# Sparse attention taken by pairs of heads, its last 16 queries gathered over heads, and the top-k rounds spread over query, key and value slots

## The chip, the cores and the metric

The kernel runs on one core of a Trainium2 chip. The metric is the device time of one execution in microseconds (us). The engines that matter here are TensorE (PE in the rows; PEld are its weight loads), VectorE (DVE), ScalarE (ACT), GpSimdE (POOL) and the queue of SyncE (SP) that fetches weights. ScalarE also issues DMAs from its own queue (ACTq).

## The reference

A network of three parts: a hybrid layer, a differential attention with a feed-forward network, and a sparse attention (DSA) with a feed-forward network. Width 1024, 512 tokens, and 16 "meta" tokens put ahead of them from the second part on, so 528 tokens. The change touches only the sparse attention:

```python
q, k, v, qi, ki, wi = jnp.split(h @ w_in, DSA_SPLITS, axis=-1)
q = apply_rope(q.reshape(B, T, 16, 64), cos, sin) * (64 ** -0.5)
k = apply_rope(k.reshape(B, T, 16, 64), cos, sin)
...
raw = jnp.einsum('bqhd,bkd->bqhk', qib, ki).astype(f32) * (64 ** -0.5)
score = jnp.einsum('bqhk,bqh->bqk', jax.nn.relu(raw), wb)
score = jnp.where(causal & (k_pos < 16)[None, :], BIG_SCORE, score)
score = jnp.where(causal, score, -jnp.inf)
top_val, top_idx = lax.top_k(score, 128)       # n_keys // 4
...                                            # keys and values at top_idx
s = jnp.where(valid[:, None], s, -jnp.inf)
p = jax.nn.softmax(s, axis=-1)
o = jnp.einsum('bhqj,bqjhd->bqhd', p, vs)
```

An indexer scores all keys for each query, the 128 best keys are taken, and 16 heads of 64 channels attend to them. Then comes the output projection, and later the second feed-forward network.

## The kernel before

**Weights in slots.** Each projection is a stream of slots: 128 output channels by 1024 inputs, 512 KB. SyncE fetches a slot into `raw`; ScalarE rounds it to `w_hi` (line 895); the rest, `w_lo`, is the difference, made by VectorE (line 1131) or, for the slots S_DSA + 7 to the first of the output projection, by GpSimdE (line 867). TensorE takes three products for each half of the tokens and each of eight input tiles (lines 551 to 553), 48 matmuls for a slot. Two slots of `w_hi` and `w_lo` exist, so ScalarE waits for the slot two back before it writes the next one (`ahead`). Three pairs of PSUM banks take the results.

**The stage ahead of the attention.** Slots S_DSA + 0 to 6 are the indexer's query, key and weights; then the indexer's scores are accumulated in `sel`, one tile of 128 queries at a time. After that TensorE runs slots 7 to 30: 8 slots of queries, 8 of keys, 8 of values. Queries and keys are made in pairs of slots: `rope` (lines 1180 to 1188) reads both from PSUM on VectorE, and `scatter` (line 939) moves the result by eight DMAs of ScalarE's queue to where its heads belong. A slot can start only when the `rope` that reads the same pair of banks three slots back is done (`dsa_free`). Value slots are scaled by VectorE (`vch`, line 1199), transposed by TensorE (line 584), and copied to `vtok` by VectorE (lines 1194, 1195).

**The top-k.** Queries stand in `TILES`: four tiles of 128 and a last one of 16, so tile n has keys(n) = 256, 384, 512, 528 keys for n = 1 to 4 (n = 0 selects nothing). One round, `take_eight(r)`, finds the eight largest of each row (MAX8, line 1476) and replaces them by a mark (line 1477); 16 rounds take 128 keys, and a final instruction (line 1480) turns the marks into a bias of 0 or -1e30. The four tiles make 64 rounds, all on VectorE, eight after each of the eight `rope`s, tile by tile in the order 1, 2, 3, 4. The value slots come when all are done.

**The attention** goes through 80 units, `HEAD_UNITS`: 16 heads by five tiles. The queries stand in `qz`, padded with zeros to 128 rows so that a head can be taken against the keys of two heads in `kz`; GpSimdE zeroes it (line 877). Of unit u TensorE makes the scores (line 596; the last tile in two halves, lines 598 and 599), VectorE scales them, adds the bias and takes the maximum (line 1309) and its negative (line 1311), ScalarE takes the exponential and its sum (line 1009), VectorE divides (lines 1317, 1319), TensorE transposes the probabilities (line 608), ScalarE copies them out (`copy_pt`, lines 946 to 949), TensorE multiplies by the values (line 618: for both heads of a pair, 128 columns), and ScalarE copies the head's 64 rows to `oT` (line 1015). TensorE computes the scores three units ahead of the transposes, VectorE and ScalarE work two units ahead. After every pair of heads ScalarE rounds `oT` to `o_hi` and GpSimdE makes the rest `o_lo` (line 873), which the output projection needs. A float32 product of TensorE appears as two instructions in the trace, a transpose as one.

The differential attention, earlier in the same kernel, takes its heads by pairs already: its scores (line 644) use 64 rows of the array for each head of a pair; its transposes are line 663 and its values line 672. The first layer has products with 64 columns of weights for each of two heads (line 1688).

## Time and profile before

| | us |
|---|---|
| median of 3 runs | 2063.96 (2061.88 to 2067.09) |
| profiled execution, its own time | 2064.38 |
| its span, first to last instruction | 2062.5 |
| TensorE busy | 1864.3 (90%) |
| VectorE busy | 1244.1 (60%) |
| ScalarE busy | 680.1 (33%) |
| GpSimdE busy | 101.4 (5%) |
| share of TensorE in the chain that ended last | 78% |
| share of VectorE in that chain | 16% |

The span is what the profile sees of the execution; 1.9 us of the execution's own time lie outside it. "Busy" is a union of instructions that overlap. The clock column of a row is the TensorE clock granted in that stretch: 1.00 is 2.4 GHz and 0.50 is 1.2 GHz, its two levels. Two lines of the chain are the rounds of the top-k: line 1477 with 2% of the span and line 1476 with 2%.

### The profile page before, as it was taken

How to read it: one execution, taken by the hardware profiler on the slowest of the kernel's cores; microseconds unless marked ns; L12 is line 12 of the kernel's file. 1: busy time of each engine (PE TensorE's matmuls, PEld its weight loads, DVE VectorE, ACT ScalarE, POOL GpSimd, SP SyncE). 2: the span in 40 equal slices, each digit the busy share in tenths (PEclk: the TensorE clock that was granted, in tenths of full speed). 3: DMA queues.
4: the chain of work that ended last, by engine and by line, in shares of the span. 5: the costliest groups of instructions: out<-in, count | busy, mean ns of one | idle time of the engine just before them, and what ended most of it. 6: DMA issues, size and time to landing. Idle time of an engine off the chain costs nothing.

```text
span 2062.5 us, 34799 instructions
## 1 busy us (share of the span) xinstructions
PE 1864.3 (90%) x14740; PEld 1659.1 (80%) x14740; DVE 1244.1 (60%) x2283; ACT 680.1 (33%) x1273; POOL 101.4 (5%) x53
## 2 busy tenths in 40 slices
PE   7999568979998859999999996987999999999996
PEld 3777458858994439999999995887766899999885
DVE  5256645437546654878773356797466477777534
ACT  3354222332115543222222223211477432222221
POOL 0000002000000000000000020232200000000000
PEclk9999769999997979999999998998999999999998
DMA  8332200022530002323333331342100123333331
GB/s 308 120 92 83 92 1 3 13 82 86 142 93 11 1 0 73 103 92 92 88 89 101 95 100 53 86 112 82 53 1 1 34 91 93 92 93 92 101 103 62
DMA packets 51290, 160.39 MB, mean 78 GB/s; under 512 B 8256, under 2 KB 9280, under 8 KB 51008
## 3 DMA queue, kind: packets, MB, share of 16 engines
q1 hardware_dynamic: 43648, 147.35, 22.9%
q10 hardware_dynamic: 7488, 10.82, 2.1%
q8 instruction: 117, 1.92, 0.4%
q14 instruction: 37, 0.30, 0.0%
HBM read 146.32 MB, written 2.10 MB: 72 GB/s over the span
## 4 chain that ended last, share of the span: by engine, by line
PE 78%; DVE 16%; issue 2%; ACT 1%; DMA 1%; ACTq 1%; SPq 0%; DVEq 0%
PE banks L551 17%; PE banks L552 17%; PE banks L553 16%; PE banks L1779 3%; PE banks L1567 3%; PE banks L1569 3%; PE banks L1568 3%; PE banks L618 3%; DVE arena L1477 2%; DVE top L1476 2%; PE banks L672 2%; PE banks L596 1%; PE banks L608 1%; DMA ring<-in_weights 1%; PE banks L644 1%
## 5 line engine op out<-in xcount | busy, mean ns | idle before, releaser
L551 PE MATMUL banks<-hn_hi,w_hi 128*128 128x264 f32 (+1 forms) x2288 | 658.9, 288 | 31.3 <-DVE hn_lo L1138 14.9
L552 PE MATMUL banks<-hn_lo,w_hi 128*128 128x264 f32 (+1 forms) x2288 | 653.1, 285 | 0.0
L553 PE MATMUL banks<-hn_hi,w_lo 128*128 128x264 f32 (+1 forms) x2288 | 652.3, 285 | 0.0
L895 ACT ACTIVATE w_hi<-raw 128x1024 fp32r<-128x1024 f32 x207 | 219.4, 1061 | 887.8 <-PE banks L553 836.3
L551 PEld LDWEIGHTS banks<-hn_hi,w_hi 128*128 128x128 f32 x2288 | 436.8, 191 | 35.8 <-issue 20.4
L552 PEld LDWEIGHTS banks<-hn_lo,w_hi 128*128 128x128 f32 x2288 | 438.2, 192 | 0.1
L553 PEld LDWEIGHTS banks<-hn_hi,w_lo 128*128 128x128 f32 x2288 | 435.6, 190 | 0.0
L1131 DVE TENSOR_TENSOR w_lo<-raw,w_hi 128x1024 fp32r<-128x1024 f32 x181 | 221.6, 1225 | 197.0 <-ACT w_hi L895 196.9
L551 PE MATMUL banks<-a_hi,w_hi 128*128 128x264 f32 (+1 forms) x528 | 169.1, 320 | 1.6 <-DVE u_in L1361 0.8
L552 PE MATMUL banks<-a_lo,w_hi 128*128 128x264 f32 (+1 forms) x528 | 169.4, 321 | 0.0
L553 PE MATMUL banks<-a_hi,w_lo 128*128 128x264 f32 (+1 forms) x528 | 169.4, 321 | 0.0
L551 PEld LDWEIGHTS banks<-a_hi,w_hi 128*128 128x128 f32 x528 | 99.5, 188 | 9.4 <-DVE u_in L1361 1.0
L553 PEld LDWEIGHTS banks<-a_hi,w_lo 128*128 128x128 f32 x528 | 99.3, 188 | 7.6
L552 PEld LDWEIGHTS banks<-a_lo,w_hi 128*128 128x128 f32 x528 | 99.1, 188 | 7.8
L1120 DVE TENSOR_TENSOR ring_r<-ring,ring_r 128x1024 fp32r<-128x1024 f32 x33 | 40.5, 1226 | 86.7 <-ACT ring_r L890 86.6
L1568 PE MATMUL banks<-h_r,ring_r 128*128 128x512 f32 x200 | 79.2, 396 | 0.0
L551 PE MATMUL banks<-o_hi,w_hi 128*128 128x264 f32 (+1 forms) x256 | 73.2, 286 | 0.0
L552 PE MATMUL banks<-o_lo,w_hi 128*128 128x264 f32 (+1 forms) x256 | 73.1, 285 | 0.0
L553 PE MATMUL banks<-o_hi,w_lo 128*128 128x264 f32 (+1 forms) x256 | 72.8, 284 | 0.0
L867 POOL TENSOR_TENSOR w_lo<-raw,w_hi 128x1024 fp32r<-128x1024 f32 x26 | 62.4, 2400 | 183.8 <-ACT w_hi L895 183.8
L618 PE MATMUL banks<-arena 128*128 128x128 f32 (+2 forms) x480 | 68.4, 272 | 0.5 <-ACT arena L1015 0.5
L1373 DVE SCALAR_TENSOR_TENSOR u_c<-u_in,cols,u_c 128x528 f32<-128x528 f32 (+1 forms) x88 | 67.0, 761 | 3.1
(370 smaller groups left out, 2955.7 us busy)
## 6 DMA issues: line engine op xcount, KB each, us to landing
raw<-in_weights SPq DMA_DIRECT2D x207, 512.0 KB, 3.6
ring<-in_weights SPq DMA_DIRECT2D x50, 512.0 KB, 4.6
arena<-arena ACTq DMA_DIRECT2D x144, 66.0 KB, 2.5
arena<-in_gate_w SPq DMA_DIRECT2D x8, 512.0 KB, 3.8
h<-in_xT SPq DMA_DIRECT2D x2, 1024.0 KB, 6.9
out_t<-h SPq DMA_DIRECT2D x4, 512.0 KB, 2.8
arena<-in_alibi SPq DMA_DIRECT2D x1, 1024.0 KB, 6.9
arena<-in_cosT ACTq DMA_DIRECT2D x2, 264.0 KB, 2.7
```

The source lines that it names most:

```text
L551: mm(o, w[0][:, j, :], x[0][:, k, lo:hi], start=first, stop=False)
L552: mm(o, w[0][:, j, :], x[1][:, k, lo:hi], start=False, stop=False)
L553: ins_ = mm(o, w[1][:, j, :], x[0][:, k, lo:hi], start=False, stop=last)
L618: last = mm(psum[:, 7, 0:w], vtok[0:kj, j, e:e + P], pt[0:kj, u % 2, j * w:(j + 1) * w], start=j == 0, stop=j == n)
L867: g.tensor_tensor(w_lo[:, w, :], raw[:, (n - S_DA) % RAW, :], w_hi[:, w, :].bitcast(F32), ALU.subtract).then_inc(S["w_split_p"], 1)
L895: nc.scalar.activation(w_hi[:, j % SPLIT, :], raw[:, j % RAW, :], ACT.Copy).then_inc(S["w_hi_done"], 1)
L1131: V.tensor_tensor(w_lo[:, w, :], raw[:, (n - S_DA) % RAW, :], w_hi[:, w, :].bitcast(F32), ALU.subtract).then_inc(S["w_split_d"], 1)
L1373: st.link(V.scalar_tensor_tensor(out=c, in0=u[:, taps[1]], scalar=w[1], in1=c, op0=ALU.mult, op1=ALU.add))
L1567: mm(out, w[0][:, k, :], x_hi, start=start, stop=False)
L1568: mm(out, w[0][:, k, :], x_lo, start=False, stop=False)
L1569: return mm(out, w[1][:, k, :], x_hi, start=False, stop=stop)
L1779: last = mm(out(s), lhs[r], rhs[r], start=start, stop=stop)
```

## The change

1. `take_eight` goes through the tiles in the order 4, 1, 2, 3. Its 64 rounds are spread by the list `ROUNDS`: 6, 5, 6, 5, 6, 5, 6, 5 after the eight `rope`s (44), and 3, 2, 3, 2, 3, 2, 3, 2 in the eight value slots (20), through the new argument `between` of `values`.
2. When tile 4 is done, ScalarE's queue copies its 16 rows of bias seven times to the other partitions, between two of its `ahead`s.
3. Queries are scattered without padding (`to_plain_q`), and `qz` isn't zeroed. The last 16 queries of all 16 heads are gathered in `qlast`, zeroed by GpSimdE (256 columns) and filled by two copies on VectorE.
4. The attention has 34 units instead of 80: two for the last 16 queries (four pairs of heads each, 32 rows a pair), then 8 pairs by 4 tiles. A pair's scores take 64 rows of the array for each head, its values 64 columns for each head; one ScalarE instruction copies the transposed probabilities of both heads, and one VectorE copy (it was ScalarE's work) moves both heads' output to `oT`.
5. The sign is folded into the scaling, so that line 1311's instruction goes.
6. TensorE now computes the scores of unit v + 2 after the transposes of unit v; before, those of unit u + 3 came ahead of the transposes of unit u.

```diff
+    LAST_UNITS = 2
+    DSA_UNITS = [(None, v) for v in range(LAST_UNITS)] + [(p, n) for p in range(8) for n in range(4)]
...
+                    for c in range(2):
+                        r = slice(64 * c, 64 * c + 64)
+                        last = mm(psum[:, 2 * (v % 2) + c, 0:keys(n)], qs[r, p, n * P:(n + 1) * P], kz[r, p, 0:keys(n)], start=True, stop=True)
...
+                    for j in range(n + 1):
+                        for c in range(2):
+                            e = p * P + 64 * c
+                            last = mm(psum[64 * c:64 * c + 64, 6 + v % 2, 0:P], vtok[:, j, e:e + 64], pt2[:, v % 2, c, j * P:(j + 1) * P],
+                                      start=j == 0, stop=j == n)
...
-            for u in range(80):
-                if u + LA_PE < 80:
-                    scores(u + LA_PE)
-                transposes(u)
-                if u:
-                    values(u - 1)
+            for v in range(N):
+                transposes(v)
+                if v + 2 < N:
+                    scores(v + 2)
+                if v:
+                    values(v - 1)
...
+            if i == 14:
+
+                act.wait_ge(S["sel_done"], 1)
+                for j in range(1, 8):
+                    act.dma_start(sel[16 * j:16 * j + 16, 3, :], sel[0:16, 3, :]).then_inc(S["sel_spread"], 16)
...
+            for v in range(N):
+                normalise(v)
+                if v + 2 < N:
+                    soft(v + 2)
+                if v:
+                    out(v - 1)
...
-            n, w = TILES[1 + r // 16]
+            n, w = TILES[(4, 1, 2, 3)[r // 16]]
...
+        ROUNDS = [(11 * i + 1) // 2 for i in range(8)] + [44 + (20 * j + 4) // 8 for j in range(8)] + [64]
```

On VectorE, in the middle of the value slots, before (line 1199 is the scaling of a slot, 1194 and 1195 its copies):

```order
L1480 TENSOR_SCALAR arena<-arena 16x528
L1199 TENSOR_TENSOR arena<-banks,rs 128x528 x2
L1194 COPY arena<-banks 128x4x128
L1195 COPY arena<-banks 16x128
L1199 TENSOR_TENSOR arena<-banks,rs 128x528
L1194 COPY arena<-banks 128x4x128
L1195 COPY arena<-banks 16x128
```

and in the changed kernel (1235 is the scaling, 1230 and 1231 the copies, 1537 and 1538 a round):

```order
L1235 TENSOR_TENSOR arena<-banks,rs 128x528
L1230 COPY arena<-banks 128x4x128
L1231 COPY arena<-banks 16x128
L1537 MAX top<-arena 128x8
L1538 MATCH_REPLACE arena<-top,arena 128x512
L1537 MAX top<-arena 128x8
L1538 MATCH_REPLACE arena<-top,arena 128x512
L1541 TENSOR_SCALAR arena<-arena 128x512
L1230 COPY arena<-banks 128x4x128
L1231 COPY arena<-banks 16x128
```

The second piece is the end of the stage: two rounds and tile 3's final instruction now stand between the last slot's scaling and its copies.

On TensorE inside the attention, before (608 transposes, 618 values, 596 scores; here a product is one row):

```order
L608 MATMUL banks<-ident,arena 128x128 x3
L618 MATMUL banks<-arena 128x128 x2
L596 MATMUL banks<-arena 128x256
L608 MATMUL banks<-ident,arena 128x128 x4
L618 MATMUL banks<-arena 128x128 x3
L596 MATMUL banks<-arena 128x384
```

and in the changed kernel (623 transposes, 610 scores, 641 values):

```order
L623 MATMUL banks<-ident,arena 128x128 x6
L610 MATMUL banks<-arena 128x128 x2
L641 MATMUL banks<-arena 64x128 x4
L623 MATMUL banks<-ident,arena 128x128 x8
L610 MATMUL banks<-arena 128x256 x2
L641 MATMUL banks<-arena 64x128 x6
```

Each row now serves two heads. Before, the scores that follow a unit's values were asked for three units ahead of their transposes; now they are those of two units on, and stand behind the transposes and ahead of the values of the unit before.

On ScalarE's queue, after the fourth `rope`, in the changed kernel (922 rounds a slot, 966 is `scatter`, 1141 the copies of tile 4's bias):

```order
L922 ACTIVATE w_hi<-raw 128x1024 x2
L966 DMA arena<-arena 32x528 x8
L1141 DMA arena<-arena 16x528 x7
L922 ACTIVATE w_hi<-raw 128x1024 x2
L966 DMA arena<-arena 32x528 x8
```

Seven DMA issues stand ahead of the rounding of the second slot in this place; before, only the eight of `scatter` did.

## Rows read from the trace of the kernel before

**Rows 1.** Stretches: us; busy us of PE, PEld, DVE, ACT, POOL; clock; DMA.
```profile
1309.46:1428.34 118.88, 99.77 (x768) 98.64 (x766) 114.00 (x244) 18.03 (x17) 40.92 (x17) 0.93 0.40 111
1472.52:1622.68 150.16, 137.50 (x912) 101.66 (x912) 92.07 (x400) 105.65 (x342) 9.16 (x8) 1.00 0.02 5
620.50:743.00 122.50, 96.11 (x593) 57.15 (x594) 79.77 (x182) 66.49 (x208) 0.00 (x0) 0.86 0.00 1
...
262.00:316.00 54.00, 31.80 (x230) 25.92 (x232) 28.90 (x46) 11.82 (x19) 0.00 (x0) 0.63 0.00 1
```

**Rows 2.** Waits of TensorE, 1309 to 1473 us: us in total, times, longest.
```profile
PE banks L551 <- DVE arena L1183: 12.9, 5, 3.9
```

**Rows 3.** Timeline of VectorE in the query and key slots: start us, us, instruction.
```profile
1321.98 0.71 DVE L1180 TENSOR_TENSOR arena<-banks,arena 128x528 f32<-128x528 f32 x1
...
1334.01 0.71 DVE L1180 TENSOR_TENSOR arena<-banks,arena 128x528 f32<-128x528 f32 x1
...
1411.86 0.71 DVE L1180 TENSOR_TENSOR arena<-banks,arena 128x528 f32<-128x528 f32 x1
...
1415.69 0.69 DVE L1476 MAX8 top<-arena 16x8 f32<-16x528 f32 x1
...
1427.89 0.42 DVE L1480 TENSOR_SCALAR arena<-arena 16x528 f32<-16x528 f32 x1
1428.34 1.32 DVE L1199 TENSOR_TENSOR arena<-banks,rs 128x528 f32<-128x528 f32 x2
```

**Rows 4.** Timeline of ScalarE and its queue: slot roundings and one scatter.
```profile
1315.26 1.07 ACT L895 ACTIVATE w_hi<-raw 128x1024 fp32r<-128x1024 f32 x1 [4.74 <-PE banks L553]
1315.27 5.01 ACTq L939 DMA_DIRECT2D arena<-arena  x8
1321.06 1.06 ACT L895 ACTIVATE w_hi<-raw 128x1024 fp32r<-128x1024 f32 x1 [4.73 <-PE banks L553]
...
1437.34 1.06 ACT L895 ACTIVATE w_hi<-raw 128x1024 fp32r<-128x1024 f32 x1 [14.10 <-PE banks L553]
...
1469.09 1.06 ACT L895 ACTIVATE w_hi<-raw 128x1024 fp32r<-128x1024 f32 x1 [5.29 <-PE banks L553]
```

**Rows 5.** Group of GpSimdE's roundings by line: count, busy us, mean ns.
```profile
L867 POOL TENSOR_TENSOR w_lo<-raw,w_hi 128x1024 fp32r<-128x1024 f32 x26 | 62.4, 2400 | 183.8 <-ACT w_hi L895 183.8
```

**Rows 6.** Timeline at the attention's start and end.
```profile
1471.50 0.69 DVE L1194 COPY arena<-banks 128x512 f32<-128x512 f32 x1 [0.92 <-PE banks L584]
...
1472.52 2.40 PE L596 MATMUL banks<-arena 128*128 128x128 f32 x8 [1.06 <-DVE arena L1195]
...
1621.40 1.36 PE L618 MATMUL banks<-arena 128*128 128x16 f32 x10 [0.45 <-ACT arena L1015]
...
1622.68 0.39 PE L551 MATMUL banks<-o_hi,w_hi 128*128 128x258 f32 x1
```

**Rows 7.** Timeline of TensorE in the differential attention: transposes, pair scores.
```profile
697.14 0.66 PE L663 MATMUL banks<-ident,arena 128*128 128x128 f32 x4 [1.11 <-DVE arena L1238]
...
698.39 0.92 PE L644 MATMUL banks<-arena 64*128 64x384 f32 x4
...
701.02 1.13 PE L644 MATMUL banks<-arena 64*128 64x512 f32 x4
...
714.29 1.65 PE L644 MATMUL banks<-arena 64*128 64x384 f32 x4
```

**Rows 8.** The same of the first layer: products with 64 columns of weights.
```profile
161.75 0.66 PE L1688 MATMUL banks<-arena 128*64 128x128 f32 x8
```

**Rows 9.** Groups of VectorE in the attention, shapes apart: count, busy us, mean ns.
```profile
L1309 DVE CUSTOM_DVE_ANT_0 arena<-banks,arena 128x512 f32<-128x512 f32 x16 | 11.1, 691 | 17.6 <-PE banks L596 17.6
...
L1319 DVE TENSOR_SCALAR arena<-arena,stat 128x512 f32<-128x512 f32 x16 | 7.8, 487 | 0.6
...
L1319 DVE TENSOR_SCALAR arena<-arena,stat 128x128 f32<-128x128 f32 x16 | 4.6, 286 | 0.6
L1309 DVE CUSTOM_DVE_ANT_0 arena<-banks,causalf 128x128 f32<-128x128 f32 x16 | 4.5, 281 | 0.6 <-PE banks L596 0.6
```

More of the change, by code:

```diff
@@ L311, in build @@
     osq = cd.take(5, P)
+    cs = Carve(arena2[:, ARENA2 - 8 * T2:ARENA2], 8 * T2)
+    pt2 = cs.take(2, 2, 4 * P)
+    prob_more = cs.take(4, T2)
+    qlast = pt.rearrange("p a b -> p (a b)")[:, 0:8 * 32].rearrange("p (k m) -> p k m", k=8)
     qiz = vtok.rearrange("p a b -> p (a b)")[:, 0:8 * T2].rearrange("p (a b t) -> p a b t", a=4, b=2)
@@ new lines, in values @@
+            def values(v):
+                p, n = DSA_UNITS[v]
+                pe.wait_ge(S["a_pt"], 40 + v + 1)
+                if v >= 2:
+                    pe.wait_ge(S["a_o"], 16 + v - 1)
+                if p is None:
+                    for g in range(4):
+                        e = (4 * n + g) * P
+                        for j, (_, kj) in enumerate(TILES):
+                            last = mm(psum[:, 6 + v % 2, 32 * g:32 * g + 32], vtok[0:kj, j, e:e + P],
+                                      pt2[0:kj, v % 2, j // 4, j % 4 * P + 32 * g:j % 4 * P + 32 * g + 32], start=j == 0, stop=j == 4)
+                else:
+                    for j in range(n + 1):
+                        for c in range(2):
+                            e = p * P + 64 * c
+                            last = mm(psum[64 * c:64 * c + 64, 6 + v % 2, 0:P], vtok[:, j, e:e + 64], pt2[:, v % 2, c, j * P:(j + 1) * P],
+                                      start=j == 0, stop=j == n)
+                last.then_inc(S["a_pv"], 1)
@@ L631, in pair_scores @@
+            N = len(DSA_UNITS)
+            for v in range(2):
+                scores(v)
+            for v in range(N):
[4 more added lines that the diff above has]
+                    values(v - 1)
+            values(N - 1)
         def pair_scores(u, masked, free):
@@ L1021, in dsa_attention, with exps @@
-            for u in range(LA_ACT):
-                exps(u)
-            for u in range(80):
-                hd, n, w = HEAD_UNITS[u]
-                if u + LA_ACT < 80:
-                    exps(u + LA_ACT)
-                copy_pt(40 + u, n, w)
-                if u:
-                    out(u - 1)
-            out(79)
+            def exps(v):
+                p, n = DSA_UNITS[v]
+                for c in range(1 if p is None else 2):
+                    act.wait_ge(S["a_max"], 40 + 2 * v + c + 1)
+                    x = dsa_prob(v, c)[:, 0:T2 if p is None else keys(n)]
+                    last = A(x, x, ACT.Exp, bias=stat[:, v % 4, c:c + 1], scale=-1.0, accum_out=stat[:, v % 4, 2 + c:3 + c])
+                last.then_inc(S["a_exp"], 1)
@@ new lines, in high @@
+            def high(p):
+                act.wait_ge(S["a_o"], 16 + LAST_UNITS + 4 * p + 4)
+                A(o_hi[:, p, :], oT[:, p, :], ACT.Copy).then_inc(S["o_hi"], 1)
+            N = len(DSA_UNITS)
+            exps(0)
+            for v in range(N):
+                if v + 1 < N:
+                    exps(v + 1)
+                copy(v)
+                p = (v - LAST_UNITS - 5) // 4
+                if p >= 0 and (v - LAST_UNITS) % 4 == 1:
+                    high(p)
+            high(7)
@@ L1203, in values @@
                     to_tokens(j - 1)
+                if between:
+                    between(j)
             to_tokens(7)
@@ new lines, in normalise @@
+            def normalise(v):
+                p, n = DSA_UNITS[v]
+                heads = 1 if p is None else 2
+                ve.wait_ge(S["a_exp"], 80 + v + 1)
+                st.link(V.reciprocal(stat[:, v % 4, 4:4 + heads], stat[:, v % 4, 2:2 + heads]))
+                for c in range(heads):
+                    x = dsa_prob(v, c)[:, 0:T2 if p is None else keys(n)]
+                    last = V.tensor_scalar(x, x, stat[:, v % 4, 4 + c:5 + c], None, ALU.mult)
+                last.then_inc(S["a_prob"], 1)
@@ new lines, in out @@
+            def out(v):
+                p, n = DSA_UNITS[v]
+                ve.wait_ge(S["a_pv"], 40 + v + 1)
+                src = psum[:, 6 + v % 2, 0:P]
+                if p is None:
+                    pairs = src.rearrange("p (g m) -> p g m", g=4)
+                    for c in range(2):
+                        r = slice(64 * c, 64 * c + 64)
+                        last = V.tensor_copy(oT[r, 4 * n:4 * n + 4, 4 * P:T2], pairs[r, :, 16 * c:16 * c + 16])
+                else:
+                    last = V.tensor_copy(oT[:, p, n * P:(n + 1) * P], src)
+                last.then_inc(S["a_o"], 1)
@@ L1328, in residual @@
+            ve.wait_ge(S["sel_spread"], 16 * 7)
+            N = len(DSA_UNITS)
+            soft(0)
+            soft(1)
+            for v in range(N):
+                normalise(v)
[3 more added lines that the diff above has]
+                    out(v - 1)
+            out(N - 1)
         def residual(v, s0, parts, base, gain=None):
```

204 lines of the change are left out of this document (97 added, 107 removed).

## The prediction

> **What bounds the kernel now.** I read first how busy each engine is in the two stages that the change touches, then what ended TensorE's waits there, then the timelines of VectorE and ScalarE, and last, for operations that the attention doesn't have yet, the same operations elsewhere in this kernel. From slot 8's end at 1309.46 us to the last round of the top-k, TensorE is busy 99.8 of 118.9 us and VectorE 114.0 [rows 1]: VectorE is the bound. TensorE lost 12.9 us waiting for `rope` to free its banks [rows 2], and its clock is 0.93 on average there, so part of the stretch ran at 1.2 GHz. In the value slots VectorE has little to do. So rounds moved there are gained, as long as VectorE keeps up. In the attention, 1472.5 to 1622.7 us, TensorE is busy 137.5 of 150.2 us at a clock of 1.00, ScalarE 105.7, VectorE 92.1 [rows 1]: here TensorE is the bound.
>
> **The change, first stage: query, key and value slots.** Undelayed, a slot takes 5.80 us (1315.26 to 1321.06), and a value slot with its transposes 6.35 (five of them from 1437.34 to 1469.09) [rows 4]. From slot 8's end there are 16 slots without transposes and 6 with them: 16 x 5.80 + 6 x 6.35 = 130.9 us. Before, 3.43 us passed from slot 30's end at 1469.09 to the attention's first scores at 1472.52 [rows 4, 6]. Now two rounds and a final instruction come in between: 2 x 1.53 + 0.45, less VectorE's wait of 0.92 that they fill [rows 3, 6], so 6.0 us.
>
> Can VectorE keep up? A `rope` takes 3.83 us (1411.86 to 1415.69). A round of tile 4 takes (1427.89 - 1415.69) / 8 = 1.53 us; one of tile 1 takes (12.03 - 3.83 - 0.3) / 8 = 0.99 [rows 3]; I take 1.25 for tile 2, between them, and 1.53 for tile 3, whose rows are as long as tile 4's. A pair of slots gives 11.6 us. The first three need 3.83 + 6 x 1.53 = 13.0, then 11.5, then 3.83 + 5 x 1.53 + 0.45 + 0.99 = 12.9 us: VectorE is 1.4, 1.3 and 2.6 us late. TensorE doesn't wait before 3.3 us of lateness, since the third slot on starts 5.8 us after the pair's end and `rope` has read its banks in about 2.5. Then come 8.8 to 9.8 us, and it catches up. A value slot with three rounds needs 3 x 1.53 + 1.6 = 6.2 of 6.35 us. So nothing is lost, by a margin of 0.7 us in one place and 0.15 in the other.
>
> ScalarE's queue needs 5.01 us for eight DMAs [rows 4], 0.63 each, so the seven new ones take up to 4.4. After slot 15's end it waits 0.6 us for the late fourth `rope`, issues 5.0 + 4.4, rounds slot 18 in 1.06, and GpSimdE splits it in 2.40 [rows 5]: 13.6 us after slot 15's end, where TensorE wants it after 11.6. That is 2.0 us of stall; nothing if short transfers issue in half the time. I take 2.0. GpSimdE's saved zeroing and the two copies into `qlast` lie beside other work: cost nothing.
>
> The stage: 130.9 + 6.0 + 2.0 = 138.9 us where before it took 1472.52 - 1309.46 = 163.1. **Gain 24.2 us**, 26 at most; 16 if rounds ran a tenth slower among their new neighbours (64 rounds are 85 us).
>
> **The attention at full clock.** The new order makes a loop. VectorE divides unit v; TensorE transposes it and only then makes the scores of v + 2; only then can VectorE take their maxima; and after that it copies the output of v - 1 and divides v + 1. Before, the scores were asked for three units ahead and nothing closed. What is queued behind VectorE's wait for the scores is the copy and the next division, for which TensorE waits. The terms, for tile n of a pair of heads:
> - Division: the reciprocal and its gap 0.2, and two of 0.286 (n = 0) to 0.487 (n = 3) [rows 9]: 0.71, 0.84, 1.02, 1.11 us.
> - Transposes: four in 0.66, of which 0.11 each and 0.22 for the end [rows 7]; on the path 2(n + 1) x 0.11 + 0.06: 0.28, 0.50, 0.72, 0.94.
> - Scores: the differential attention's pairs, 0.92 for 384 keys and 1.13 for 512 [rows 7]: 0.49, 0.70, 0.92, 1.13. Two heads cost what one costs today.
> - Maxima: two of 0.281 to 0.691 [rows 9]: 0.50, 0.79, 1.06, 1.32.
> - Values, beside the maxima: eight products with 64 columns in 0.66 [rows 8]: 0.44, 0.66, 0.88, 1.10 for 4, 8, 12, 16 of them.
> - The copy of the output, 0.22 (a copy of 512 is 0.69), and 0.09 for the two handovers.
>
> Unit n meets the scores of tile n + 2 and the values of tile n - 1. n = 0: 0.71 + 0.28 + 0.92 + 1.10 + 0.31 = 3.32. n = 1: 0.84 + 0.50 + 1.13 + 1.32 + 0.31 = 4.10. n = 2: 1.02 + 0.72 + 0.49 + 0.66 + 0.31 = 3.20. n = 3: 1.11 + 0.94 + 0.70 + 0.88 + 0.31 = 3.94. **A pair takes 14.6 us**, eight 117. ScalarE isn't late: all its work before was 105.7 us [rows 1], and it loses the copies. The two units of the last queries: 40 value instructions each at 0.13 (ten in 1.36 [rows 6]) are 5.2 us, and nothing is in flight yet. Scores 1.2, maxima 1.6, division 0.7, transposes 0.8, scores 0.5, maxima 0.5, division 0.7, transposes 0.8, scores 0.7, values 5.2, copies 0.4: 13.1 until the loop starts, and 4.1 in its first turn, where the second of them does its values. The scores with 32 columns are the weakest price: up to 3.5 us a unit if nothing shares the array. Sum 134 us, which against 150.2 would be a gain of 16.
>
> **What the clock makes of it.** In this loop TensorE works 8.8 of 14.6 us, 60%, with a pause of 1 to 2 us in every unit. Two stretches of the trace have such pauses. The differential attention, busy 78%, ran at a mean clock of 0.86, so 28% of its time at 1.2 GHz; the stretch 262 to 316 us, busy 59%, at 0.63, so 74% [rows 1]. At 1.2 GHz the scores of 384 keys took 1.65 in place of 0.92 [rows 7]; with TensorE's terms times 1.8 a pair takes 5.15 + 5.40 + 4.70 + 5.95 = 21.2 us. I take half of the time at either level, between the two stretches: the mean rate gives 2 / (1/14.6 + 1/21.2) = 17.3 us a pair, 138.4 for eight, 155.6 with the first two units. **Loss 5.4 us.** At 28% the attention takes 145, at 74% 169.
>
> The sum: 2064.4 (the profiled execution's own time, 0.4 over the median) - 24.2 + 5.4 = **2045.6 us**.
>
> The Trainium skill's page TensorE: Matmul & The Clock Gate (Part 1) says that the gate's default is the lower rate and that activity lifts it. The rows above agree: the dense attention of before stands at 1.00, the stretches with pauses lower; no term rests on the page.
>
> **The rivals.**
> - The clock holds better, as in the differential attention (28% low) or fully: 2064.4 - 24.2 - 5 = 2035, or 2024. For it: half clock fills the pauses, and a full stretch brings the clock back. Against: here no unit is without a pause.
> - The clock is low for 74%: 2064.4 - 24.2 + 19 = 2059.
> - On the other side: it stays low throughout. Eight pairs take 170, the attention 187, and the time is 2077. It decides from about 83% of the attention at 1.2 GHz, where 24.2 us are used up. For it: at 1.2 GHz a pair still has 5.6 us of pauses in 21.2; against: the stretch with the most pauses had a quarter of its time at the upper level.
> - Changing the array's shape costs. Three times a unit TensorE goes between 64 rows, the full array and 64 columns. If each time it had to run empty, at the 0.2 us that the end of a group has in [rows 7, 8], that is 3 x 34 x 0.2 = 20 us: 2066. Against it: the differential attention's scores start as their predecessors' last instruction is ending, with no such gap in its prices of 0.92 and 1.13 [rows 7].
> - VectorE doesn't keep up in the first stage, rounds a tenth slower: gain 16, 2054.
>
> The fourth of these is a rule of the Trainium skill, TensorEngine Tiling (Array Packing), Key Properties: "Mode switching requires drain". By the rule the time would be that 2066, by the rows 2045.6.
>
> **How the numbers follow.** Low for about half: 0.42. Low for 28% or less: 0.33. For 74%: 0.11. Throughout: 0.06. Run empty: 0.04. VectorE late: 0.04. The range leaves out the upper end of the second, full clock, and the dearest: 2026 to 2062. A measurement of this kernel can tell 0.3%, 6 us. Faster by more than that: the first, the second, the last, and half of the third, 0.84. Within it: the rest of the third, and running empty, 0.09. Slower: 0.07.
>
> **What would show it.** In the profile of the changed kernel: slots every 5.8 us with the clock at 1.00 up to the value slots, and no wait of TensorE for `rope`; one stall of about 2 us near the fourth `rope`; value slots every 6.35; 6 us from the last slot to the attention; a clock well under 1.00 in the attention, which takes 145 to 169 us; VectorE waiting for the scores in every unit. I am wrong if a pair at full clock isn't near 14.6 us, if the clock stays up, or if TensorE waits for VectorE again in the slots.

## The result, and the profile after

The changed kernel takes 2071.26 us (median of 20 runs, 2064.18 to 2076.77); the kernel before took 2063.94 beside it (20 runs, 2060.26 to 2067.47). The ratio is 1.0033, 95% interval 1.0023 to 1.0043: **slower by about 7 us, where 2045.6 us and a gain were forecast.** The profiled run is the fastest of the 20, 2064.18 us with a span of 2062.1, so a second profile was taken later (2074.45 us, span 2072.4).

Stretches of the first profile. Columns as in [rows 1]: stretch; busy us of PE, PEld, DVE, ACT, POOL; granted clock; DMA share and GB/s.
```profile
1307.51:1448.83 141.32, 133.49 (x1088) 132.49 (x1087) 124.17 (x258) 23.23 (x23) 52.56 (x22) 0.99 0.41 117
1454.92:1622.26 167.34, 117.84 (x730) 79.58 (x730) 64.64 (x267) 67.76 (x175) 9.13 (x7) 0.74 0.00 1
1461.70:1492.30 30.60, 27.16 (x105) 21.69 (x107) 4.83 (x22) 4.94 (x16) 0.00 (x0) 0.50 0.00 1
1504.07:1521.05 16.98, 11.24 (x77) 7.11 (x77) 7.65 (x32) 8.14 (x21) 1.30 (x1) 0.80 0.00 0
```
The first answers to the slots of before (the first of [rows 1] goes to the last round, this one to slot 30's end), the second to the attention of before, 150.2 us at clock 1.00. With the 6.1 us between, the first stage takes 147.4 us (forecast 138.9, before 163.1) and the attention 167.3 (forecast 155.6, before 150.2). The third line is most of the attention's start, wholly at 1.2 GHz, as were its first 3.3 us too; the fourth is one pair of heads in the steady loop.

The same columns in the second profile: the whole attention, two of its stretches, and in the last line one pair of heads wholly at 1.2 GHz.
```profile
1458.73:1632.61 173.88, 124.92 (x731) 83.22 (x731) 64.80 (x267) 67.77 (x175) 9.11 (x7) 0.68 0.00 1
1465.60:1512.90 47.30, 39.84 (x171) 29.83 (x171) 11.30 (x47) 11.46 (x35) 0.00 (x0) 0.50 0.00 0
1588.00:1615.00 27.00, 20.18 (x102) 12.55 (x100) 9.98 (x44) 10.36 (x27) 1.30 (x1) 0.50 0.00 0
1589.65:1610.94 21.29, 15.85 (x76) 9.47 (x77) 7.73 (x32) 8.15 (x21) 1.30 (x1) 0.50 0.00 0
```
The two profiles differ by 10.3 us: 6.5 are in the attention, where the half clock at the start lasts 47.3 instead of 30.6 us and one piece of it near the end is 27 us long; 3.4 lie ahead of slot 8's end; 0.4 in the slots. Slot 8 ends at 1307.51 in the first of them and at 1309.46 in the profile of the kernel before; over all the profiles of this study that moment lies between 1305.0 and 1314.6 us. The total of a single profile carries that scatter, so stages are compared by their own lengths.

What TensorE waited for from slot 8's end to the attention in the first profile (us in total, times, longest):
```profile
PE banks L560 <- POOL w_lo L894: 5.9, 2, 4.5
PE banks L605 <- DVE arena L1231: 3.6, 1, 3.6
PE banks L560 <- DVE arena L1219: 1.6, 1, 1.6
```
The 12.9 us of waits for `rope` [rows 2] are 1.6 now. In their place stands GpSimd's split of a slot, 4.5 us at once. Its cause stands on ScalarE and its queue:
```profile
1348.11 1.06 ACT L922 ACTIVATE w_hi<-raw 128x1024 fp32r<-128x1024 f32 x1 [4.74 <-PE banks L562]
1352.84 5.13 ACTq L966 DMA_DIRECT2D arena<-arena  x8
1358.01 4.44 ACTq L1141 DMA_DIRECT2D arena<-arena  x7
1362.55 1.06 ACT L922 ACTIVATE w_hi<-raw 128x1024 fp32r<-128x1024 f32 x1 [13.38 <-PE banks L562]
```
The seven small DMAs (L1141) take 4.44 us, as forecast, behind the scatter of the fourth `rope`, which starts only at 1352.84, 4.7 us after slot 15's end at 1348.11, where the forecast had 0.6. Slot 18's rounding waits 13.4 us. That `rope` was late because three operations of VectorE were long. They are L1223 at 1310.16, L1541 and L1223 at 1349.61 (L1541 ends tile 4's rounds, L1219 and L1223 are `rope`); GpSimd's splits stand below them:
```profile
1310.16 1.46 DVE L1223 TENSOR_TENSOR arena<-arena 128x528 f32<-128x528 f32 x1
...
1344.21 1.92 DVE L1541 TENSOR_SCALAR arena<-arena 16x528 f32<-16x528 f32 x1
...
1348.88 0.70 DVE L1219 TENSOR_TENSOR arena<-banks,arena 128x528 f32<-128x528 f32 x1
1349.61 2.58 DVE L1223 TENSOR_TENSOR arena<-arena 128x528 f32<-128x528 f32 x1
```
```profile
1343.45 2.39 POOL L894 TENSOR_TENSOR w_lo<-raw,w_hi 128x1024 fp32r<-128x1024 f32 x1 [3.41 <-ACT w_hi L922]
...
1349.25 2.38 POOL L894 TENSOR_TENSOR w_lo<-raw,w_hi 128x1024 fp32r<-128x1024 f32 x1 [3.40 <-ACT w_hi L922]
```
L1223 takes 0.71 alone; here it began 0.36 us after a split and ended 0.56 after the split's end at 1351.63. L1541 took 0.42 before [rows 3] and 1.92 here. The three are 0.75, 1.50 and 1.87 us longer than alone, 4.1 us together, which is the step from 0.6 to 4.7.

The same could be read from the trace of before. There one of `rope`'s last two operations (L1187, L1188; 0.71 and 0.70 us alone) also met a split in places, and once it was the split that got longer (2.82 us in place of 2.40), where L1188 had begun 0.14 us ahead of it:
```profile
1312.11 1.47 DVE L1187 TENSOR_TENSOR arena<-arena 128x528 f32<-128x528 f32 x1
...
1351.06 0.70 DVE L1188 TENSOR_TENSOR arena<-arena 128x528 f32<-128x528 f32 x1
1351.20 2.82 POOL L867 TENSOR_TENSOR w_lo<-raw,w_hi 128x1024 fp32r<-128x1024 f32 x1 [3.40 <-ACT w_hi L895]
```
The forecast took `rope`'s price from the one at 1411.86, which no split met.

A second stall, which the forecast didn't have, stands at slot 25. Slot 23 ended at 1402.76 (5.80 behind slot 22's end at 1396.96), but the eighth scatter held ScalarE's queue and with it slot 25's rounding:
```profile
1401.95 5.35 ACTq L966 DMA_DIRECT2D arena<-arena  x8
1407.41 2.21 ACT L922 ACTIVATE w_hi<-raw 128x1024 fp32r<-128x1024 f32 x2 [9.39 <-issue]
```
From slot 22's end to slot 25's at 1417.07 pass 20.11 us where 2 x 5.80 + 6.35 = 17.95 were due: 2.2 us are lost.

The attention's start on TensorE (L605 and L635: scores and values of the last queries; L610, L623: pairs):
```profile
1454.92 3.60 PE L605 MATMUL banks<-arena 128*32 128x264 f32 x32 [3.65 <-DVE arena L1231]
...
1464.89 9.70 PE L635 MATMUL banks<-arena 128*128 128x32 f32 x40
...
1475.85 0.69 PE L623 MATMUL banks<-ident,arena 128*128 128x128 f32 x2 [1.27 <-DVE arena L1361]
...
1478.05 9.69 PE L635 MATMUL banks<-arena 128*128 128x32 f32 x40
1489.14 1.11 PE L623 MATMUL banks<-ident,arena 128*128 128x128 f32 x4 [1.40 <-DVE arena L1361]
```
The forecast had 5.2 us for each 9.70, and 13.1 from the start to the loop, which took 20.9 (1454.92 to 1475.85). One unit of the steady loop, at full clock:
```profile
1521.05 0.44 PE L623 MATMUL banks<-ident,arena 128*128 128x128 f32 x2 [0.99 <-DVE arena L1361]
1521.41 0.92 PE L610 MATMUL banks<-arena 64*128 64x384 f32 x4
...
1522.26 1.09 PE L641 MATMUL banks<-arena 128*64 128x128 f32 x16
1522.49 0.56 DVE L1351 CUSTOM_DVE_ANT_0 arena<-banks,arena 128x384 f32<-128x384 f32 x1 [1.50 <-PE banks L610]
...
1523.84 0.62 DVE L1361 TENSOR_SCALAR arena<-arena,stat 128x256 f32<-128x256 f32 x2
...
1524.51 0.66 PE L623 MATMUL banks<-ident,arena 128*128 128x128 f32 x4 [1.16 <-DVE arena L1361]
```
The loop is there as forecast: transposes, scores, values, each starting just before the modelled end of its predecessor; VectorE waits for the scores, TensorE for the division. The unit takes 3.46 us (forecast 3.32).

### The profile page after: what moved, and what is told of

It reads as the page before. It is cut to its first block, busy times and chain, and to the rows that moved or that the text cites. A ratio compares the mean times of both kernels' runs of the same rounds, so it can differ in the third digit from the quotient of the medians.

```text
span 2062.1 us, 33968 instructions
## 1 busy us (share of the span) xinstructions
PE 1837.7 (89%) x14558; PEld 1629.3 (79%) x14558; DVE 1220.8 (59%) x2153; ACT 642.2 (31%) x1105; POOL 94.3 (5%) x53
## 4 chain that ended last, share of the span: by engine, by line
PE 80%; DVE 15%; issue 2%; ACT 1%; ACTq 1%; DMA 1%; POOL 0%; SPq 0%; DVEq 0%
PE banks L560 17%; PE banks L561 17%; PE banks L562 17%; PE banks L1856 3%; PE banks L1644 3%; PE banks L1646 3%; PE banks L1645 3%; PE banks L697 2%; PE banks L623 2%; PE banks L610 1%; DVE arena L1361 1%; PE banks L641 1%; ACTq L966 1%; PE banks L635 1%; PE banks L669 1%
## 5 line engine op out<-in xcount | busy, mean ns | idle before, releaser
L623 PE MATMUL banks<-ident,arena 128*128 128x128 f32 x160 | 32.2, 349 | 46.7 <-DVE arena L1361 46.7
```

Source lines behind the costliest of these rows:

```text
L623: last = nc.tensor.transpose(psum[:, 4 + c, j * P:(j + 1) * P], dsa_prob(v, c)[:, j * P:(j + 1) * P], ident[:, :])
```

## The experiments

Times are medians; ratios are to the kernel before, measured on the same chip beside each group.

**e1, the rounds alone** (kernel before; new `ROUNDS`, three rounds between value slots; old order of tiles, old attention).
```
+ for r in range(ROUNDS[i], ROUNDS[i + 1]): take_eight(r)
+ values(S_DSA, 23, 8, False, rounds_between)
```


> The kernel before with one thing changed: the 64 rounds of the top-k spread as in the changed kernel (44 after the ropes, 20 in the value slots), tiles in their old order, the attention as before. Theory (the first stage gives what was forecast, less the stall of the seven DMAs, which this kernel doesn't have): the stage from slot 8's end to the attention takes 137 to 140 us instead of 163, the attention 150, the time is 2064 - 24 = 2040 us. Rival (VectorE doesn't keep up, because its own instructions are stretched beside GpSimdE's splits): TensorE waits for ropes again, the gain is 10 to 16 us, 2048 to 2054 us.

2048.96 us (4 runs), ratio 0.9919 [0.9903, 0.9936]. The time is the rival's, but its reason isn't: no wait for `rope` is left. The stage takes 141.9 us (1311.48 to 1453.35), 21.2 less than before. This profile is 14.7 us shorter than that of before: of the 21.2 us, 6.5 are given back outside the stage, 2.0 ahead of slot 8's end, 2.0 in the attention (152.2) and 2.5 behind it. So spreading the rounds is worth 21 us in its stage and 15 in the time. The changed kernel's stage is 5.5 us longer than this one; e3 accounts for 4.1 of them.

**e2, the change without its rounds** (changed kernel, eight rounds to each `rope` again; the seven DMAs and the new order of the tiles stay).
```
- ROUNDS = [(11 * i + 1) // 2 for i in range(8)] + [44 + (20 * j + 4) // 8 for j in range(8)] + [64]
+ ROUNDS = [8 * i for i in range(8)] + [64] * 9
```


> The changed kernel with the rounds put back: eight after each rope, none in the value slots; all else as changed. Theory (the new attention costs 17 us more than the old one, and the spread rounds hid that): 2071 + 16 = 2087 us or a little less, attention near 167 us. Rival (the attention is not slower, the changed first stage is what disappoints): the time is at or under 2064 us.

2087.5 us (4 runs), ratio 1.0116 [1.01, 1.0132]. In the slots TensorE waits for VectorE again:
```profile
PE banks L560 <- DVE arena L1219: 16.1, 4, 6.8
PE banks L593 <- DVE arena L1235: 6.3, 1, 6.3
```
The stage and the attention:
```profile
1309.26:1479.29 170.03, 143.18 (x1097) 141.34 (x1096) 132.15 (x270) 25.68 (x24) 54.74 (x23) 0.92 0.34 97
1479.29:1643.80 164.51, 115.46 (x731) 78.49 (x731) 64.72 (x267) 67.76 (x175) 9.12 (x7) 0.74 0.01 4
```
The rest of the change costs 23 us, and 23 less the 15 of e1 is 8: the measured +7 is the sum of its parts. Not all of the 23 are the attention's. In this profile it is 14.4 us longer than before, and the stage 7.0 (170.0 for 163.1), where the seven DMAs and the new order of the tiles are what is left of the change. Over three profiles (this and the changed kernel's two) the attention lost 14, 17 and 24 us where 5.4 were forecast.

**e3, the seven small DMAs behind the last `rope`** (moved in ScalarE's queue from ahead of slot 18 to ahead of slot 28).
```
-            if i == 14:
+            if g == 25:
                 act.wait_ge(S["sel_done"], 1)
                 for j in range(1, 8): act.dma_start(sel[16*j:16*j+16, 3, :], sel[0:16, 3, :])
```


> The changed kernel with the seven DMAs of tile 4's bias issued in the value slots, after the rounding asked for at slot 25, instead of between two roundings of the key slots. Theory (they delayed ScalarE's rounding, and the 6 us stall at slot 18 and the 3.4 us of low clock behind it are theirs): no wait of TensorE for GpSimdE's split there, 8 us faster than the changed kernel, 2063 us. Rival (the late rope delays the rounding anyway, the DMAs matter little): within 2 us of the changed kernel, 2069 to 2073 us.

2066.1 us (10 runs), ratio 1.0009 [0.9999, 1.0018]. The stage and the attention:
```profile
1314.61:1457.91 143.30, 134.67 (x1096) 133.18 (x1095) 130.09 (x270) 25.58 (x24) 55.02 (x23) 0.99 0.41 118
1457.91:1628.98 171.07, 122.13 (x730) 81.52 (x731) 64.69 (x267) 67.78 (x175) 9.11 (x7) 0.70 0.00 1
```
The stage is 4.1 us shorter than the changed kernel's 147.4: 6.1 are won at slot 18, where no wait for the split is left, and 2.0 lost again at slot 25, where the stall is now 4.2. The medians differ by 5 us, between theory (8) and rival (2). The attention took 3.7 us more than in the changed kernel's first profile, at a clock of 0.70 for 0.74, so a single profile can't show this gain.

**e4, scores ahead of the transposes** (changed kernel; scores of v + 2 issued before the transposes of v).
```
 for v in range(N):
-    transposes(v)
     if v + 2 < N: scores(v + 2)
+    transposes(v)
```


> The changed kernel with TensorE's order in the attention turned: the scores of unit v + 2 ahead of the transposes of unit v, nothing else. Theory (the loop from division to transposes to scores to maxima makes the attention long and holds the clock low): VectorE no longer waits for scores, a pair takes 11 to 12 us instead of 17, the clock is above 0.9 in the attention, the attention takes 110 to 125 us, and the time is 2020 to 2030 us. Rival (the length is that of the pairs' own work on VectorE and ScalarE, or the clock stays low whatever the order): a pair stays at 15 us or more, 2055 us or more.

2034.05 us (4 runs), ratio 0.9845 [0.9829, 0.9861]; the attention takes 134.4 us. Two lines exchanged give 37 us over the changed kernel, so the closed loop cost more than all that the attention lost. The theory is right in that, and wrong in the other half: the clock stayed at 0.74 where over 0.9 was expected, and the attention missed its 110 to 125 us. So this gain is not one of the clock. A pair wholly at full clock takes 11.88 us, where the closed loop's takes 14.5 (e5):
```profile
1550.20:1562.08 11.88, 8.81 (x77) 5.42 (x77) 8.60 (x32) 7.69 (x22) 1.40 (x1) 1.00 0.01 1
```

**e5, the loop's pauses filled** (changed kernel, four unused products behind each unit's values).
```
+ for f in range(4):
+     mm(psum[:, 6 + v % 2, 384:512], ident[:, :], ident[:, :], start=True, stop=True)
```


> The changed kernel with four products of the identity matrix by itself (128 columns each, into 128 unused columns of the bank of the value products) added behind every unit's value products, 136 in all; their result is read by nobody, and nothing is left out of the computation. In the changed kernel a pair takes 17.0 us, of which 10.2 pass at the full clock and 6.8 at half, and TensorE waits 46.7 us in all for VectorE's normalisation ahead of the transposes. Theory: the half clock follows TensorE's idle time in the loop, so that with its gaps filled the clock stays full: a pair then takes 14.6 us (the loop's own time at full clock) to 15.5 (if a third of the added work isn't covered by the waits), attention 137 to 144 us instead of 167.3, the time 2038 to 2047 us. Rival: the clock doesn't go by the gaps and the added products only add, 0 to 3.4 us a pair: 2066 to 2095 us.

2042.68 us (4 runs), ratio 0.9892 [0.9877, 0.9907]. The attention and a pair:
```profile
1458.73:1600.89 142.16, 128.39 (x1002) 94.01 (x1002) 63.86 (x267) 67.78 (x175) 9.17 (x7) 0.93 0.01 2
1498.71:1513.25 14.54, 13.05 (x109) 9.28 (x108) 7.54 (x32) 8.15 (x21) 1.31 (x1) 1.00 0.00 1
```
More work for TensorE, and 29 us less time. A pair takes 14.54 us at clock 1.00: the forecast's 14.6 for full clock. With TensorE's pauses filled the mean clock rose from 0.74 to 0.93, and the half clock had cost the attention 25 us (against the first profile's 167.3) to 32 (against the second's 173.9). The value products of the first last-query unit took 5.44 us here, those of the second 7.11, partly at half clock.

**e6 and e7: e3 and e4 together, and with the last queries' units inside the loop** (units 6 and 15 of the list instead of 0 and 1).
```
- DSA_UNITS = [(None, v) for v in range(LAST_UNITS)] + [(p, n) for p in range(8) for n in range(4)]
+ DSA_UNITS = [(p, n) for p in range(8) for n in range(4)]
+ DSA_UNITS.insert(6, (None, 0))
+ DSA_UNITS.insert(15, (None, 1))
```


> The changed kernel with the scores of two units ahead issued before the transposes (as in the run that had that alone: 2034.1 us) and with the seven small DMAs of the mask moved behind the last rope (in the run that had that alone the stage from slot 8's end to the attention's start took 143.3 us against 147.4). Theory: the two save independently: 2034.1 - 4.1 = 2030 us, the first stage 143.3 us, the attention 134.4 us. Rival: what the stage gives back is lost to the clock in the attention's start, as it was when moved alone: 2034 us with an attention of 138 us or more.

> The same two edits, and the two units of the last queries in the middle of the loop (one between two units of the second pair, one in the fourth pair) instead of ahead of it. Theory: ahead of the loop each of them waited at half clock (scores 1.8 us, values 9.7 and 10.3 us against 5.2 at full clock); in the loop their values take 5.2 to 6.5 us and cover the VectorE and ScalarE chain of their neighbours, so that the attention loses 6 to 10 us: 2020 to 2026 us, the attention 125 to 129 us. Rival: the clock falls behind them just the same, wherever they stand: within 2 us of the run with the two edits (2028 to 2034), values at 9 to 10 us each.

e6: 2023.58 us (4 runs), 0.9808 [0.9785, 0.983]. e7: 2016.64 (4 runs), 0.9765 [0.9749, 0.9782]; its attention takes 125.8 us. The gains of e3 and e4 add up (5 and 37 us would give 2029), and the place of the two units gives 7 us more; both kernels are faster than their theories had it, by 6 and 3 us.

**The changed kernel once more**, for the profile shown above.

> The changed kernel once more, for its profile: its 20 runs lie between 2064.2 and 2076.8 us, the profiled one at the lower end with a mean clock of 0.926, and those with 0.920 at 2070 to 2077. Theory: the 7 us between them are a further stretch of half clock of about 14 to 27 us, in the attention (as one stood at 1516 to 1543 us in the run with the DMAs moved) or ahead of slot 8 (there 7 us later). Rival: no such stretch, the time lost in waits: then the clock's low time is the same within 3 us.

2074.45 us: the theory. By the mean clocks 0.68 and 0.74, 111 us of the attention were at 1.2 GHz here and 87 in the first profile, 24 us more; the rest of the difference lies ahead of slot 8's end.

**e8, GpSimd's subtractions doubled** (changed kernel, slots 10 to 23).
```
 g.tensor_tensor(w_lo[:, w, :], raw[...], w_hi[...], ALU.subtract).then_inc(S["w_split_p"], 1)
+if S_DSA + 10 <= n < S_DSA + 24:
+    g.tensor_tensor(pt2[:, 0, :, :], h[:, 0:2, 0:4 * P], h[:, 2:4, 0:4 * P], ALU.subtract)
```


> The changed kernel, in which GpSimd does after each of 14 splits (slots 10 to 23 of the layer) one more subtraction of two 128x1024 operands of SBUF into an unused place of SBUF, of about 2.4 us; VectorE, ScalarE and TensorE run what they ran, and nothing is left out. Theory (a): VectorE's operations from SBUF to SBUF are stretched while GpSimd subtracts: the rope's two closing operations (0.71 us alone, 1.46 or 2.58 where they met a split) and the rounds' 128x256 scalings (0.42 alone, 1.92 once) are then stretched about twice as often, by 1 to 2.5 us a slot pair, VectorE's busy time from slot 8's end to slot 30's end rises by 4 us or more over the 124.2 of the changed kernel, while MAX8, MATCH_REPLACE and the four operations that read PSUM keep their length; the stage becomes 2 to 8 us longer. Rival (b): the long ones were waits for something else (a semaphore, the DMAs of the ropes): VectorE's busy time there stays within 1 us of 124.2.

2088.28 us (one run); the stage takes 165.15 us instead of 147.4. Its busy times, and single lines of VectorE in it (ns: shortest, median, longest; L1228 closes `rope`, L1541 is MAX8):
```profile
1308.05:1473.20 165.15, 141.07 (x1100) 139.23 (x1101) 148.09 (x270) 25.56 (x24) 91.33 (x37) 0.95 0.36 102
```
```profile
L1228 DVE TENSOR_TENSOR arena<-arena x8: 694/2888/2914, 1312.1 to 1419.1; 128x528 f32<-128x528 f32 x8
L1541 DVE MAX8 top<-arena x40: 407/560/700, 1314.9 to 1419.7; 16x8 f32<-16x528 f32 x16, 128x8 f32<-128x256 f32 x16, 128x8 f32<-128x384 f32 x8
```
The same two in the changed kernel, where L1224 closes `rope` and L1537 is MAX8:
```profile
L1224 DVE TENSOR_TENSOR arena<-arena x8: 694/699/703, 1311.5 to 1401.2; 128x528 f32<-128x528 f32 x8
L1537 DVE MAX8 top<-arena x50: 408/561/700, 1312.2 to 1418.6; 16x8 f32<-16x528 f32 x16, 128x8 f32<-128x256 f32 x16, 128x8 f32<-128x384 f32 x16, 128x8 f32<-128x512 f32 x2
```
Theory (a) holds and was sized too small: VectorE's busy time rose by 18.3 us (from 129.8 over the same part), the stage by 17.7. Operations with two operands in SBUF go from 0.70 to 2.9 us beside a subtraction of GpSimd's; MAX8 doesn't change at all. A part of the 17.7 is not this: a split can now wait behind an added subtraction, and the clock in the stage is 0.95 for 0.99.

**e9, the last queries inside the loop, alone** (changed kernel with the lists of e7).

> The changed kernel with one edit: the two units of the last queries stand in the middle of the loop (one inside the second pair, one inside the fourth) and not ahead of it. It tells what the attention's start costs. Theory: the 20.9 us from the attention's start to the loop's first transposes (20.7 in the second profile of the changed kernel), against 13.1 + 4.1 that the prediction gave the two units, came of the half clock, in which the value products of each take 9.7 us in place of 5.2; in the loop they run at full clock for at least half of their time: attention 158 to 163 us instead of 167.3, time 4 to 9 us below the changed kernel's. Rival: the two units cost the same wherever they stand, since they leave the clock at half themselves: attention 166 to 170 us, time within 2 us of the changed kernel's.

2072.71 us (10 runs), ratio 1.0039 [1.0028, 1.005]: the changed kernel's time. The attention takes 173.2 us, and both value products are as slow as before:
```profile
1492.98 9.70 PE L638 MATMUL banks<-arena 128*128 128x32 f32 x40
...
1544.20 9.70 PE L638 MATMUL banks<-arena 128*128 128x32 f32 x40
```
The rival holds: in this loop the clock is at half around these units in both places tried. With the scores first their place did matter (e7, 7 us under e6).

**e10 and e11, two and four unused products behind each unit of e7's kernel.**

> The fastest kernel so far (scores issued first, small DMAs late, last queries in the middle: 2016.6 us, a pair at 12.8 us with the clock at half in 51 us of the attention) with two unused products of the identity by itself behind each unit (1.8 us of TensorE's time a pair). Theory: the clock stays full in most of the attention, as with four of them in the changed kernel (a pair at 14.54 us, the loop's own time), and a pair takes 12.0 to 12.6 us: 2010 to 2015 us. Rival: with the scores first the loop has 1.4 us of waits a pair instead of 5.8, so that there is little to fill: the added products cost what they take, 1.8 us a pair less what the clock gives: 2017 to 2028 us.

> The same with four unused products behind each unit (3.6 us of TensorE's time a pair). TensorE's needed work in a pair is about 9.5 us at full clock (14.54 us less 1.4 of waits and 3.6 of added products in the kernel that had them), so that with four added ones it is 13.1: theory, full clock throughout and a pair of 13.1 to 13.8 us, 2018 to 2025 us, slower than with two. Rival: only four hold the clock and two don't: then this one is the faster of the two.

e10: 2023.42 us (4 runs), 0.9795 [0.9776, 0.9815]; e11: 2028.84 (4 runs), 0.9818 [0.9802, 0.9835]. The clock rises (0.88 and 0.92 in the attention, e7 0.79), but the time grows by 7 and 12 us: the rival of e10. e11 is slower than e10, as its theory had it, but above its 2018 to 2025. The attention takes 128.3 and 135.9 us, where this kernel without them takes 125.8 (e7) and 121.3 (e13). Of these two loops, filling paid in the one where TensorE stood idle for 49 of 167 us, not in the one where it did for 19 of 126.

**e12, the output's split on VectorE** (e7's kernel; eight subtractions of 128x528 taken from GpSimd, and done by VectorE behind the last unit of the next pair), **and e13, e7's kernel beside it.**
```
-        output_rests(8)
+                if v - 4 in PAIR_DONE[:7]:
+                    output_rest(PAIR_DONE.index(v - 4))
```


> The fastest kernel (scores first, small DMAs late, last queries in the middle) in which the split of the attention's output, eight subtractions of 128x528 in SBUF, is done by VectorE behind the first unit of the pair after next and not by GpSimd. Theory: beside GpSimd's split (1.3 to 1.4 us, started by ScalarE's rounding just ahead of the third unit's normalisation) that normalisation takes 1.80 us instead of 0.75, on the path to the transposes, once a pair; without it a pair falls from 12.8 us by up to 1.0, and VectorE's own 0.7 us for the split stand where TensorE doesn't wait for it: pair 11.8 to 12.4 us, attention 119 to 123 us instead of 125.8, time 2009 to 2014 us. Rival: the normalisation is not what TensorE waits for, or VectorE's 0.7 us cost as much as they save: pair 12.6 to 13.2 us, time 2014 to 2020 us.

> The fastest kernel again, beside the one before it: 2016.6 us as before by either theory (2015 to 2021).

e12: **2011.1 us** (4 runs, 2009.12 to 2016.44), 0.9745 [0.973, 0.976], by its median the fastest kernel of this study. e13: 2015.03 (4 runs, 2009.87 to 2023.8), 0.9774 [0.9752, 0.9797]; the intervals overlap, so the total alone doesn't settle it. The attention takes 116.9 us in e12's profile and 121.3 in e13's, and the rows show where. In e13, the third unit's division beside GpSimd's split, and the wait behind it:
```profile
1533.30 1.79 DVE L1362 TENSOR_SCALAR arena<-arena,stat 128x384 f32<-128x384 f32 x2
1533.47 1.40 POOL L903 TENSOR_TENSOR o_lo<-arena,o_hi 128x528 fp32r<-128x528 f32 x1 [12.74 <-ACT o_hi L1057]
...
1535.15 0.87 PE L626 MATMUL banks<-ident,arena 128*128 128x128 f32 x6 [2.12 <-DVE arena L1362]
```
In e12, without it:
```profile
1525.22 0.75 DVE L1361 TENSOR_SCALAR arena<-arena,stat 128x384 f32<-128x384 f32 x2
...
1526.02 0.87 PE L626 MATMUL banks<-ident,arena 128*128 128x128 f32 x6 [1.08 <-DVE arena L1361]
```
1.79 becomes 0.75 and the wait 2.12 becomes 1.08. One pair at full clock, first of e13 and then of e12:
```profile
1529.00:1540.88 11.88, 8.81 (x77) 5.42 (x77) 8.60 (x32) 7.44 (x20) 1.40 (x1) 1.00 0.00 1
```
```profile
1520.92:1532.37 11.45, 8.81 (x77) 5.42 (x77) 8.22 (x34) 7.69 (x21) 0.00 (x0) 1.00 0.00 0
```
The pair is 0.43 us shorter and not 1.04, because VectorE's own 0.70 us for the split cost a wait of 0.76 at the next unit. Eight pairs give 3.4 of the attention's 4.4 us; for the rest the clock (0.85 for 0.84) is a candidate that wasn't separated.

## Why the prediction was wrong

- **Slots of 5.8 us, no wait for `rope`**: right, but for 1.6 us. **6.0 us from the last slot to the attention**: 6.1. Also right that VectorE bounded the stage of before: e1, which changes only its rounds, is 21.2 us shorter there.
- **"That is 2.0 us of stall"**: failed. (Its own terms give 13.5 and 1.9 rather than 13.6 and 2.0, which changes nothing.) The DMAs' 4.4 us were right (4.44), but the scatter ahead of them was to start 0.6 us after slot 15's end and started 4.7 after it. TensorE came to slot 18 6.3 us late (1.6 of them the wait for `rope`), and half clock behind it (a mean clock of 0.51 from 1366.0 to 1369.5) cost 1.7 more: from slot 15's end to slot 18's 8.2 us were lost. The step beneath it is the one that priced `rope` and the rounds by single rows: it let GpSimd's splits lie beside VectorE at no cost. The three long operations above are the 4.1 us by which the fourth `rope` was later than forecast, and e8 shows that it is GpSimd's work that stretches them. e3 shows what the DMAs' place cost: 4.1 us in the stage.
- **"So nothing is lost" in the other slots**: 2.2 us were, at slot 25, behind the eighth scatter, whose delay of a rounding the sum left out. With 16 x 5.80 + 6 x 6.35 = 130.9 this makes the stage: 130.9 + 8.2 + 2.2 + 6.1 = 147.4, 8.5 us longer than forecast. Its gain is 15.7 instead of 24.2.
- **A pair of 14.6 us at full clock, 21.2 at half**: right, 14.54 in e5 and 21.29 in the second profile. **17.3 with half the time at either level**: near, 16.98 us in the steady part of the first profile, at a mean clock of 0.80, so at half for 40% of the time and not for 50.
- **"nothing is in flight yet ... 13.1 until the loop starts, and 4.1 in its first turn"**: the term that was mis-sized. All its parts were taken at full clock while the loop behind it was taken at half for half its time. The mean clock from the attention's start to the end of the first pair (1454.92 to 1504.07) was 0.58, with 30.6 us at 1.2 GHz in one piece. The start took 20.9 instead of 13.1, the first pair with its extra 28.2 instead of 21.4 (1475.85 to 1504.07); the seven other pairs took 2.9 less than forecast (118.2 for 121.1): 7.8 + 6.8 - 2.9 = 11.7 us, the whole miss of the attention. e5 shows that it was the clock: 5.44 us for the products that took 9.70. The -2.9 is luck of the clock in this execution: in the second profile the attention took 6.5 us more.
- **One clock for all runs**: the forecast took the mix of a typical run, and the profiled run was the kindest. The second profile has 0.68 in the attention and is 10.3 us longer. In the profile the miss is 18.6 us: 8.5 and 11.7, less 2.0 because slot 8 ended that much earlier than in the profile of before, which is luck; 0.4 are roundings and time outside the span. The median lies 7.1 us above the profile, which makes the 25.7 in all.
- **The rivals.** The clock low for 74% of the attention, forecast at 2059 us with a chance of 0.11, is the one that came nearest: the second profile's 0.68 is 64% low. With the stage's 8.5 us it would have been 2068. The rival of a slow VectorE, 2054, had the right engine but not the mechanism: MAX8 and its partner, which make the rounds, kept their length. The rival of an array that must run empty at each change of shape, 0.2 us each time, finds no support: a pair has twelve such changes, 2.4 us by that price, and took 14.54 us where 14.6 were forecast without them; and in the steady unit the scores start 0.08 us before the transposes' modelled end, and the values 0.07 before the scores'. The page TensorEngine Tiling (Array Packing) of the Trainium skill, Key Properties, asks for a drain at such a change; no row here shows a cost of it.
- **The range** reached to 2062 with each uncertainty taken by itself. The two that failed, VectorE's stage and the clock, both push the same way, and together they pass its end: 8.5 and 11.7 us on 2045.6 are 2066.
- What the prediction did not ask at all: whether the loop was needed. It described the order that closes it (transposes before the scores) and priced it; e4, which opens it, is worth 37 us. That is a chance missed, not an error of the sum.

## What to carry to other kernels

Where a dependency runs through three engines and back, ask which instruction of the next turn stands behind it in program order: issuing the independent work first (here the scores) was worth more here than any other edit, 37 us. Price the start of such a loop at the same clock as the loop. And before an engine's work is put at "beside other work", look whether its partners get longer while it runs, by the shortest and longest duration of each line, not by the mean. Here the trace of before already had 0.71 and 1.82 us for one line.

## What the runs showed of the hardware

**VectorE beside GpSimd.** Two kinds of VectorE operations that met a GpSimd subtraction in SBUF ended behind it: subtractions and additions of two SBUF operands (0.71 us became 1.46, 2.58 and 2.9) and scalings from SBUF to SBUF (0.42 became 1.92, two divisions of 0.75 together became 1.79). Operations with one operand in PSUM (0.70 in every case), MAX8 (0.41 to 0.70) and MATCH_REPLACE8 (0.41 to 0.68 with and without e8's added work) weren't touched. Where VectorE's L1188 had begun first, GpSimd's subtraction took 2.82 us instead of 2.40 (kernel before, 1351.20). The Trainium skill's page SBUF — State Buffer, section SBUF: two separate sides, calls the port pair that the two engines share an exclusive lock: of a GpSimd operation and a VectorE operation with two SBUF inputs or in a two-port mode, the one that starts first has it for its whole instruction. The traces agree, with those numbers.

**The clock as part of the loop.** The same instructions ran at a mean clock of 0.74 or 0.68 from run to run, 6.5 us apart, and adding 136 useless products to a loop with pauses made the kernel 29 us faster (e5), while adding 68 to the tighter loop made it 7 us slower (e10). The same pair of heads took 21.29 us wholly at 1.2 GHz and, with e5's added products, 14.54 wholly at 2.4: not twice as long, since part of it is VectorE's work (busy for 7.73 and 7.54 us of them).

**Small DMAs on ScalarE's queue.** Seven transfers of 16 rows took 4.44 us of issue, 0.63 each, as much each as the eight of a scatter with 32 rows (5.13 in all): the short transfers weren't issued faster.

**Open**: why the clock differs between executions of one program; how much of e8's 17.7 us came from splits that waited behind the added subtractions and how much from the clock; and why the mean clock stayed at 0.74 in e4, where TensorE stood idle for 21 of 134 us and not for 49 of 167.
